# The entry of an mLSTM: the norm ahead of it computed per token column in the feed-forward, its gate products on two column halves, two key units moved ahead of the maxima's spread

## The reference, cut to what matters

```python
# end of second_block
    h = _rmsnorm(x, norm_ffn_g[i])
    x = x + _conv_ffn(h, ff_w_up[i], ff_conv_w[i], ff_conv_b[i], ff_w_down[i])
return _rmsnorm(x, final_norm_g)      # x * rsqrt(mean(x*x) + 1e-6) * g

# start of third_block
    u = x @ w_in + b_in               # no norm of its own
    (mq, mk, mv, mo, mi, mf, ...) = split(u)
    qk = silu(causal_depthwise_conv(concat([mq, mk])))      # 4 taps
    h_a = mlstm(mq, mk, mv, mi, mf)   # 4 heads of 512; mi, mf: one gate each per head and token
```

## Time and profile before

| | us |
|---|---|
| median of 3 runs | 4210.19 |
| lowest, highest | 4194.76, 4210.41 |
| the profiled execution's own time | 4198.78 |
| its span | 4196.7 |
| TensorE, mean granted clock over the span | 0.963 of 2.4 GHz |

### The profile page before, as it was taken

How to read it: one execution, slowest core, us unless ns; L and a number is a source line. 1 busy time by engine, 2 the same in 40 slices (tenths; PEclk the granted TensorE clock), 3 DMA queues, 4 the chain that set the end, 5 groups by cost and what they waited for, 6 DMA issues and landing times. The chain is left out here.

```text
span 4196.7 us, 63027 instructions
## 1 busy us (share of the span) xinstructions
PE 3916.5 (93%) x26294; PEld 3051.8 (73%) x26294; DVE 2283.2 (54%) x3292; ACT 1308.5 (31%) x2105; POOL 1311.3 (31%) x521
## 2 busy tenths in 40 slices
PE   8999999998989998978888999899999999999998
PEld 6855788756658887567775788667777877887886
DVE  5746577366647665558875666465542426242024
ACT  3345334233204332434444333222222111103222
POOL 1011444323204441000001344345554343663442
PEclk9999999999999999989988999989999999999998
DMA  5310222222112222441112122211121121322221
GB/s 170 127 54 21 100 100 100 104 93 90 60 61 100 100 85 99 161 161 44 44 44 86 61 100 100 81 67 68 73 81 65 66 86 51 117 84 85 95 100 61
DMA packets 43598, 361.33 MB, mean 86 GB/s; under 512 B 4484, under 2 KB 4868, under 8 KB 24029
## 3 DMA queue, kind: packets, MB, share of 16 engines
q1 hardware_dynamic: 43356, 357.86, 23.5%
HBM read 334.25 MB, written 23.07 MB: 85 GB/s over the span
## 5 line engine op out<-in xcount | busy, mean ns | idle before, releaser
L335 POOL TENSOR_TENSOR ffn_weights_low<-weight_ring,ffn_weights_high 128x2048 fp32r<-128x2048 f32 x128 | 590.2, 4611 | 789.7 <-ACT ffn_weights_high L424 789.0
L192 PE MATMUL banks<-ffn_in_high,ffn_weights_low 128*128 128x512 f32 x2048 | 802.7, 392 | 20.0 <-POOL ffn_weights_low L335 6.7
L194 PE MATMUL banks<-ffn_in_high,ffn_weights_high 128*128 128x512 f32 x2048 | 799.7, 390 | 0.0
L193 PE MATMUL banks<-ffn_in_low,ffn_weights_high 128*128 128x512 f32 x2048 | 799.6, 390 | 0.0
L192 PEld LDWEIGHTS banks<-ffn_in_high,ffn_weights_low 128*128 128x128 f32 x2048 | 386.3, 189 | 104.8 <-POOL ffn_weights_low L346 11.8
L193 PEld LDWEIGHTS banks<-ffn_in_low,ffn_weights_high 128*128 128x128 f32 x2048 | 386.5, 189 | 81.0 <-issue 0.7
L194 PEld LDWEIGHTS banks<-ffn_in_high,ffn_weights_high 128*128 128x128 f32 x2048 | 386.2, 189 | 81.2
L424 ACT ACTIVATE ffn_weights_high<-weight_ring 128x2048 fp32r<-128x2048 f32 x128 | 245.1, 1915 | 561.3 <-PE banks L194 561.3
L3530 POOL TENSOR_TENSOR third_weights_low<-weight_ring,third_weights_high 128x1024 fp32r<-128x1024 f32 x144 | 364.0, 2528 | 11.5
L565 DVE SCALAR_TENSOR_TENSOR ffn_gate<-ffn_up,columns_sb,ffn_gate 128x511 f32<-128x511 f32 (+1 forms) x132 | 273.1, 2069 | 161.0 <-ACT ffn_value L467 161.0
L3528 POOL CAST third_weights_high<-weight_ring 128x1024 fp32r<-128x1024 f32 x144 | 158.1, 1098 | 550.3 <-PE banks L194 501.7
(11 more groups left out here) (600 smaller groups left out, 7343.3 us busy)
## 6 DMA issues: line engine op xcount, KB each, us to landing
weight_ring<-weights SPq DMA_DIRECT2D x144, 2048.0 KB, 7.7
scan_in<-rwkv_operands SPq DMA_DIRECT2D x7, 1280.0 KB, 7.5
rwkv_operands<-rwin_staged SPq DMA_DIRECT2D x24, 256.0 KB, 2.2
scan_in<-rwkv_operands SPq DMA_DIRECT2D x8, 512.0 KB, 4.0
bias_tiles<-bias_rows SPq DMA_DIRECT2D x8, 448.0 KB, 8.9
residual<-x SPq DMA_DIRECT2D x4, 512.0 KB, 7.2
filt_decay<-decay SPq DMA_DIRECT2D x1, 2048.0 KB, 8.1
rwkv_residual<-residual SPq DMA_DIRECT2D x1, 2048.0 KB, 7.1
```

The lines of the kernel that those rows point to most:

```text
L192: pe.matmul(out, w[1], x[0], start=start, stop=False, skip_group_check=True)
L193: pe.matmul(out, w[0], x[1], start=False, stop=False, skip_group_check=True)
L194: return pe.matmul(out, w[0], x[0], start=False, stop=stop, skip_group_check=True)
L335: pool.tensor_tensor(parts[1], landed, parts[0].bitcast(F32), ALU.subtract).then_inc(S["split"], 1)
```

## The change

It does the following.

- **`feed_forward(..., root=True)`** for `ffn3`: ScalarE squares each tile of `G.x` when it has been added, and VectorE adds the squares of 7 tiles to one tile `square_sum` between the additions. TensorE then sums over the channels with the tile as the stationary operand and one column of ones as the moving one: 4 products for `square_sum` and 4 for the last square, so that the tokens come to lie on the partitions, 4 columns of 128. Mean, root and reciprocal are taken on 128x4 (`G.roots`).
- **`norm_in_place` is gone.** The mLSTM begins with `root_spread`: 4 products that spread the 4 columns over all partitions (bank 7). VectorE scales the tiles out of that bank, and ScalarE's high parts and the gate products follow tile by tile (`x_scaled`).
- **Gate products**: for each k the two gates after each other, one to partitions 0 to 3 and one to partitions 64 to 67 of bank 4. `w_if` now lies in the constants that are loaded when the kernel starts, so that TensorE waits for no load.
- **Order on TensorE**: two key units (`columns(0, 1, range(2))`) stand ahead of the spread of the maxima, which uses banks 0 to 3 in place of 4 to 7; the other two follow it without waiting for ScalarE's copies. That wait (`spread_done` 5) stands ahead of the first value unit.
- **Order on VectorE and ScalarE**: the memsets of the bias rows lie behind the magnitude, their copies on ScalarE behind the logarithm, their split on VectorE behind the negated maxima; both engines wait for the loads (`loaded` 48) only there.

```diff
+def root_spread(pe, G, bank, spread):
+    for j in range(JT):
+        of = G.roots[:, j:j + 1]
+        of = bass.AP(tensor=of.tensor, offset=of.offset, ap=[of.ap[0], [0, P]])
+        mm = pe.matmul(G.banks[:, bank, j * P:(j + 1) * P], of, G.con("ident"), start=True, stop=True)
+    mm.then_inc(spread, 1)
...
 # feed_forward, TensorE
+            if root:
+                pe.wait_ge(S["out_squares_added"], KT - 2)
+                for j in range(JT):
+                    pe.matmul(G.banks[:, 4 + j, 0:1], square_sum[:, j * P:(j + 1) * P], G.con("ones")[:, 0:1], start=True, stop=False)
+                pe.wait_ge(S["out_squared"], KT)
+                for j in range(JT):
+                    mm = pe.matmul(G.banks[:, 4 + j, 0:1], sq[:, 3, j * P:(j + 1) * P], G.con("ones")[:, 0:1], start=False, stop=True)
+                mm.then_inc(S["out_sums"], 1)
...
 # feed_forward, ScalarE
+            if root:
+                for n, m in enumerate((*range(4, KT), *range(4))):
+                    act.wait_ge(S["added"], n + 1)
+                    act.activation(sq[:, m, :], G.x[:, m, :], ACT.Square).then_inc(S["out_squared"], 1)
+                act.wait_ge(S["out_mean"], 1)
+                act.activation(G.roots[:, :], G.roots[:, :], ACT.Sqrt).then_inc(S["out_root"], 1)
...
 # feed_forward, VectorE
+            def square_total(n):
+                dve.wait_ge(S["out_squared"], n + 1)
+                if n > 1:
+                    dve.wait_ge(S["out_squares_added"], n - 1)
+                dve.tensor_tensor(square_sum, sq[:, order[0], :] if n == 1 else square_sum, sq[:, order[n], :], ALU.add)\
+                   .then_inc(S["out_squares_added"], 1)
...
+                if root and n > 1:
+                    square_total(n - 1)
+            if root:
+                dve.wait_ge(S["out_sums"], 1)
+                dve.tensor_scalar(G.roots[:, :], G.banks[:, 4:4 + JT, 0:1].rearrange("p j o -> p (j o)"), 1.0 / D, EPS, ALU.mult, ALU.add)\
+                   .then_inc(S["out_mean"], 1)
+                dve.wait_ge(S["out_root"], 1)
+                dve.reciprocal(G.roots[:, :], G.roots[:, :]).then_inc(S["out_inverse"], 1)
+                dve.wait_ge(S["out_inverse"], 1)
...
 # second_block
-    feed_forward(G, "ffn3", "ff_norm_1", "ff_taps_1", ACT.Silu, 1)
-    norm_in_place(G, "final2", "final_norm_2")
+    feed_forward(G, "ffn3", "ff_norm_1", "ff_taps_1", ACT.Silu, 1, root=True)
...
 # mlstm, TensorE
-            pe.wait_ge(S["loaded"], 64)
-            for n in range(2):
-                for k in range(KT):
+            root_spread(pe, G, 7, S["root_spread"])
+            for k in range(KT):
+                pe.wait_ge(S["x_scaled"], k + 1)
+                for n in range(2):
                     at = k * 2 * M_HEADS + n * M_HEADS
-                    mm = pe.matmul(G.banks[0:M_HEADS, 4 + n, :], wif[:, at:at + M_HEADS], G.x[:, k, :], start=(k == 0), stop=(k == KT - 1))
-                mm.then_inc(S["if_sum"], 1)
+                    side = n * (P // 2)
+                    mm = pe.matmul(G.banks[side:side + M_HEADS, 4, :], wif[:, at:at + M_HEADS], G.x[:, k, :], start=(k == 0), stop=(k == KT - 1))
+                    if k == KT - 1:
+                        mm.then_inc(S["if_sum"], 1)
             columns(0, 0)
+            columns(0, 1, range(2))
             pe.wait_ge(S["rows_done"], 1)
-            pe.wait_ge(S["if_done"], 2)
+            pe.wait_ge(S["biased"], 4)
...
-                bank = 4 + h % 3
+                bank = h % 3
...
-            pe.wait_ge(S["rows_split"], 2)
-            pe.wait_ge(S["picked"], 1)
             for h in range(M_HEADS):
-                columns(h, 1)
+                columns(h, 1, range(4) if h else range(2, 4))
+                if h == 0:
+                    pe.wait_ge(S["rows_split"], 2)
+                    pe.wait_ge(S["picked"], 1)
                 tokens(h, 0, "v_sum")
...
 # mlstm, VectorE
-            dve.memset(gate_rows[:, :, :].bitcast(F32), 0.0).then_inc(S["rows_zeroed"], 1)
-            dve.memset(T.brows[:, :].bitcast(F32), 0.0).then_inc(S["rows_zeroed"], 1)
...
+            dve.wait_ge(S["root_spread"], 1)
+            for k in range(KT):
+                dve.scalar_tensor_tensor(out=G.x[:, k, :], in0=G.x[:, k, :], scalar=G.col("final_norm_2", k), in1=G.banks[:, 7, :],
+                                         op0=ALU.mult, op1=ALU.mult).then_inc(S["x_scaled"], 1)
...
             dve.wait_ge(S["if_done"], 2)
             dve.scalar_tensor_tensor(out=ab, in0=fg, scalar=-1.0, in1=fg, op0=ALU.mult, op1=ALU.max).then_inc(S["magnitude"], 1)
+            dve.memset(gate_rows[:, :, :].bitcast(F32), 0.0).then_inc(S["rows_zeroed"], 1)
+            dve.memset(T.brows[:, :].bitcast(F32), 0.0).then_inc(S["rows_zeroed"], 1)
+            dve.wait_ge(S["loaded"], 48)
             dve.wait_ge(S["log_done"], 1)
```

More of the change, by code:

```diff
@@ L268, in norm_scale, with feed_forward @@
                              op0=ALU.mult, op1=ALU.mult).then_inc(N["scaled"], 1)
-def feed_forward(G, name, gain, taps, act_func, shift=0, keep=1.0, norms=()):
+def feed_forward(G, name, gain, taps, act_func, shift=0, keep=1.0, norms=(), root=False):
     nc = G.nc
@@ L1538, in layer_embedding @@
         G.first += 3
[L1541 to L1561, removed]
 def first_block(G):
@@ L3516, in lay_third @@
     L.column("m_conv", six.transpose(2, 1, 0).reshape(P, 6 * 32))
-    L.column("m_if_bias", np.stack([b[8192:8196], b[8196:8200]], 1))
+    L.constant("w_if", L.matrix(w[:, 4 * M_WIDTH:4 * M_WIDTH + 2 * M_HEADS]))
+    gate_bias = np.zeros((P, 1), np.float32)
+    gate_bias[0:M_HEADS, 0], gate_bias[P // 2:P // 2 + M_HEADS, 0] = b[8192:8196], b[8196:8200]
+    L.column("m_if_bias", gate_bias)
     L.vector("m_gain", a["m_norm_g"][0])
@@ L3542, in mlstm @@
     with ExitStack() as ctx:
-        S = stage(G, "mlstm", ctx, "loaded", "if_sum", "if_done", "magnitude", "exp_done", "log_done", "step", "rows_done",
+        S = stage(G, "mlstm", ctx, "root_spread", "x_scaled", "loaded", "if_sum", "if_done", "magnitude", "exp_done", "log_done", "step", "rows_done",
                   "floor_in", "floor_done", "pairs_sum", "spread_sum", "spread_done", "x_high", "x_split", "rows_zeroed", "rows_rounded", "rows_split",
@@ L3572, in _ @@
         def _(sp):
-            sp.dma_start(wif[:, :], G.aps["w_if"]).then_inc(S["loaded"], 16)
             sp.dma_start(masks[:, :], G.aps["third_masks"]).then_inc(S["loaded"], 16)
@@ L3618, in tokens @@
                 pe.wait_ge(S["biased"], 8 * h + 4 * s + 4)
+                if h == s == 0:
+                    pe.wait_ge(S["spread_done"], M_HEADS + 1)
                 for u in range(4):
@@ L3710, in _ @@
             for k in range(KT):
+                act.wait_ge(S["x_scaled"], k + 1)
                 act.activation(T.x_high[:, k, :], G.x[:, k, :], ACT.Copy).then_inc(S["x_high"], 1)
-            act.wait_ge(S["loaded"], 64)
+            for n, to in enumerate((ig, fg)):
+                side = slice(n * (P // 2), n * (P // 2) + M_HEADS)
+                act.wait_ge(S["if_sum"], n + 1)
+                act.activation(to, G.banks[side, 4, :], ACT.Identity, bias=G.col("m_if_bias")[side, :]).then_inc(S["if_done"], 1)
+            act.wait_ge(S["magnitude"], 1)
+            act.activation(ab, ab, ACT.Exp, scale=-1.0).then_inc(S["exp_done"], 1)
+            act.wait_ge(S["exp_done"], 1)
+            act.activation(ab, ab, ACT.Ln, bias=1.0).then_inc(S["log_done"], 1)
+            act.wait_ge(S["loaded"], 48)
             act.activation(T.pick[:, :], masks[:, SEQ + P:SEQ + P + M_HEADS * P], ACT.Copy).then_inc(S["picked"], 1)
@@ L3717, in _ @@
                 act.activation(T.brows[at:at + M_HEADS, :], brows[at:at + M_HEADS, 2, :], ACT.Copy).then_inc(S["rows_rounded"], 1)
-            for n, to in enumerate((ig, fg)):
-                act.wait_ge(S["if_sum"], n + 1)
-                act.activation(to, G.banks[0:M_HEADS, 4 + n, :], ACT.Identity, bias=G.col("m_if_bias", n)[0:M_HEADS, :]).then_inc(S["if_done"], 1)
-            act.wait_ge(S["magnitude"], 1)
-            act.activation(ab, ab, ACT.Exp, scale=-1.0).then_inc(S["exp_done"], 1)
-            act.wait_ge(S["exp_done"], 1)
-            act.activation(ab, ab, ACT.Ln, bias=1.0).then_inc(S["log_done"], 1)
             act.wait_ge(S["edges"], 1)
@@ L3825, in _ @@
             dve.sem_inc(S["rows_done"], 1)
+            dve.wait_ge(S["rows_rounded"], 4)
+            for low, of in ((gate_rows[32:32 + M_HEADS, :, :], brows[32:32 + M_HEADS, 0:2, :]), (T.brows[32:32 + M_HEADS, :], brows[32:32 + M_HEADS, 2, :])):
+                dve.tensor_tensor(low, of, low.bitcast(F32), ALU.subtract).then_inc(S["rows_split"], 1)
             convolve(0, 0)
```

24 lines of the change are left out of this document (11 added, 13 removed).

## The result

The changed kernel took 4172.5 us (median of 5 runs, 4166.0 to 4183.9) against 4210.2 us before. The ratio is 0.9925, 95% interval 0.9909 to 0.9940: faster by 0.75%, which is 31.5 us, with an interval of some 6 to 7 us to either side (the medians lie 37.7 us apart and the means 34.0 us). The forecast was 4169 and a gain of 33.6 us.

What follows compares the result with a forecast made beforehand. TensorE, busy 93%, gains only where it stands or runs slowly: from ffn3's last addition to the first value unit, 5.9 + 16.1 + 27.3 + 5.5 + 11.9 = 66.7 us for 100.3. Mean 4203.5 less 33.6 gives 4169.9; 80% range 4156 to 4184.

Steps and rivals of the forecast that it cites:

- To the first scaling: From ffn3's last addition to the first scaling: 5.9 us in place of 18.6, scalings still to come.
- T0: The start of the first scaling, from which the prediction counts its positions.
- Gate products: Scalings and gate products at the mLSTM's start: 9.7 us of overlapping pairs, first at 1.2 GHz, ending at T0+10.4.
- Low parts: VectorE's eight low parts of x take 9.99 us, end at T0+15.4; unit 0 ends at T0+16.1.
- Units 1 to 5: Five column units on TensorE ahead of the maxima's spread: 5.45 us each, ending at T0+43.4.
- Row chain: Magnitude to negated maxima takes 25.4 us; rows ready at T0+40.8, 2.6 us before TensorE arrives.
- The rival of a late chain: GpSimd hits delay the rows of maxima; TensorE waits, clock falls: 9 us more, 4179; chance 0.15.
- Spread: Spread of the maxima on TensorE: 5.5 us, starting at the high clock, bounds 4.5 and 9.0.
- Units 6 and 7: Two units behind the maxima's spread: 10.9 us plus 1 us for the clock, whose bounds are 0 and 2.3.
- The rival of column halves that don't overlap: Gate product pairs of 4 columns don't overlap: first value unit 7.1 us later, 4177; chance 0.10.
- The gain that is given back later: Half the gain lost behind the passage, for instance by convolutions colliding with GpSimd: 4187; chance 0.09.
- The slower rival: TensorE stays at 1.2 GHz over the first units, 5.45 us more each: 4225; chance 0.02.

Runs made afterwards that it cites:

- The wide spread: Changed kernel with the maxima's spread products using 128 rows (124 zero) in place of 4; passage 64.9 us against 68.1, rest 3.1 us longer.
- the experiment: Changed kernel with all 16 gate products on partitions 0 to 3, in two banks; gate products 16.50 us for 9.60, passage 75.0 us.
- fillers: Changed kernel with unread products in TensorE's gaps between ffn3's last product and the gate products; passage 65.2 us against 68.1, 62.0 and 62.6 with the wide spread too.
- two edits: The wide spread alone and the fillers alone, each against the changed kernel; last addition to kernel end 1458.5 us each, against 1458.6.
- the norm apart: Changed kernel with the norm a stage of its own again, on 512 columns, ahead of the mLSTM; passage 78.8 us against 68.1.

## Why the prediction was right

The bound was read rightly: the gain came from stretches in which TensorE stood or ran at 1.2 GHz, and of the 32.0 us only 2.0 were lost again behind the passage. By the steps of the prediction:

1. *To the first scaling*: 5.9 forecast, 6.3 measured. The totals hid between the additions as they do in `ffn4` (0.68 and 0.69 us in turn). The eight one-column products took 2.3 us (2724.12 to 2726.43) for 2.1, and the start of the block the rest (0.5 us for 0.3).
2. *Gate products*: end at T0+10.4 forecast, T0+10.4 measured (2740.2 less 2729.8). The three parts of it held: 1.2 GHz at the start, the clock back 5.2 us after work resumed (5.3 taken; at 0.50 for 5.2 of the 9.60 us gives the window's mean of 0.73), and overlapping pairs. The forecast says elsewhere that the clock came back within 5 us at each of three places, though its own figure for `ffn4` is 5.9. The overlap was taken from products of 64 columns and is true of 4 columns.
3. *Low parts*: end at T0+15.4 forecast, T0+12.2 measured, 6.98 us for eight instead of 9.99. The step was mis-sized: I let two of GpSimd's subtractions meet them; GpSimd started late in the block, its first subtraction (2731.50) ran beside the scalings, which read a bank and were not stretched (5.36 us for eight), and only the second (2734.92) met a low part. The path was wrong with it: the forecast let the last low part end unit 0 at T0+16.1, and it ended at T0+15.8, by the gate products, which started it at T0+10.3. That the two ends lie 0.3 us apart is luck. GpSimd's timeline and the low parts' line in the changed kernel:

```profile
2730.38 1.04 POOL L3546 CAST third_weights_high<-weight_ring 128x1024 fp32r<-128x1024 f32 x1 [22.75 <-issue]
...
2731.50 2.36 POOL L3548 TENSOR_TENSOR third_weights_low<-weight_ring,third_weights_high 128x1024 fp32r<-128x1024 f32 x1
...
2734.92 2.35 POOL L3548 TENSOR_TENSOR third_weights_low<-weight_ring,third_weights_high 128x1024 fp32r<-128x1024 f32 x1
```

```profile
L3827 DVE TENSOR_TENSOR third_x_low<-residual,third_x_high x8: 677/678/2768, 2735.1 to 2741.4; 128x512 fp32r<-128x512 f32 x8
```

4. *Units 1 to 5*: as forecast, 27.2 us at 1.00.
5. *Row chain*: ready at T0+37.1 in place of T0+40.8, since it started earlier with the low parts, and took 24.9 us for 25.4. Cover 6.1 us in place of 2.6. The rival of a late chain had its mechanism right: 2.71, 2.20, 2.70 and 2.71 us stand in the chain of the changed kernel, each beside a subtraction of GpSimd's. But it needed more hits than before, and four such operations of over 2 us stand in the chain of before as well (2757.01, 2761.67, 2767.07 and 2772.83), so the length stayed what it was.
6. *Spread*: 4.9 forecast as 5.5.
7. *Units 6 and 7*: 11.9 forecast, 13.7 measured. This is the term that missed, and its bound too (13.2): the clock stayed low for the first 5.7 us of these units (6.6 us in all), longer than the 4.4 us of before. The wide spread shows that the narrow products are the cause; why the low stretch is longer than before it does not show.

Sum 66.7 forecast, 68.1 measured: 0.4 and 1.8 us more in steps 1 and 7, less 0.6 in step 6 and 0.2 in steps 2 to 5. Together with the 2.0 us of the rest, the gain by profiles is 30.0 us, and by the timed runs 31.5. The rival of column halves that don't overlap would have cost the 6.9 us that the experiment gave (7.1 worked out). The gain that is given back later is true to 2 us, by the clock and not by the convolutions that it was pinned on: the last of these ended at 2808.8, before the scores needed them. The slower rival never appeared.

What was luck: the absolute time. 4169 rests on the mean of four executions; a single one can lie 10 us to either side for reasons that lie ahead of `ffn3`. What makes those executions differ there stays open. In the two profiles of before and after, 7.7 us arise ahead of the first feed-forward and about as much again in the scan of the second block; no run here looked into them.

## What to carry to other kernels

- Where executions differ by more than a change is worth, put the change between two marks in the trace and compare that stretch: here it repeated to 0.1 us (0.6 with fillers) while single executions differed by some 20. Then add up to the end as well: two edits that each gained 3 us between the marks gained nothing up to the last instruction.
- When TensorE has to wait for a chain of small operations, count the clock on both sides of the gap. A gap of 4.75 us cost 8.0 in the passage. Thin products at the end of a busy stretch cost 3.2 us in and behind them; padding them with zero rows took that away there, and alone it brought nothing in all, since the clock was lost at two later gaps.
- Undo each part alone. The four edits of this change were worth 11, 8, 7 and 3 us in the passage, and the trace shows for each which wait or which stretch of low clock came back.

## What the runs showed of the hardware

- Four float32 products with 4 rows, then 14 small transposes (5.0 us in all, TensorE busy throughout) were followed by a clock of 0.50 for 6.6 us, and for about 3.4 us in the kernel with the norm apart. With 128 rows it stayed at 1.00. Products of 4 columns but 128 rows brought the clock back (gate products, 5.2 us after they began).
- The clock behind one and the same gap is not the same in every variant: behind 3.7 to 3.9 us it stayed at 0.50 for some 3 us in nine profiles and for some 6 in four, and behind 1.97 us it stayed at 1.00 in the same nine and fell in the same four.
- Two float32 products on column halves 0 and 64 run at the same time even with 4 columns each: 9.60 us for 16, against 16.50 on one half, both from a start at 0.50.
- GpSimd's first work in the mLSTM came 2.7 us behind VectorE's (2730.38 and 2727.65), with 35 semaphores to clear, and 0.5 us behind it before the change, with 6; with the norm apart, again 6, it was 0.7 us (2743.07 and 2742.40). The prediction had counted some 38 for the 35.
- VectorE operations that read one operand from a bank ran their normal 0.67 us beside GpSimd's subtractions, those with two operands from the on-chip memory were stretched to up to 2.77 us, and so were some with one (2.20 us at 2752.91). Of those with two the Trainium skill says so in "SBUF — State Buffer", SBUF: two separate sides; this trace agrees with it.
